# The rests of 25 weight units computed by Pool instead of VectorE in a two-block transformer kernel

## The chip, the cores and the metric

The kernel runs on one core of one Trainium2 chip. The metric is the device time of one execution in microseconds (us). The kernel before has a median of 2389.01 us in 3 runs (2388.89 to 2389.41).

## The reference

Two hybrid transformer layers are applied to one sequence of 512 positions and 1024 channels, all in fp32. The part that matters here is the sparse branch of the first layer's attention, and the projections that are computed beside it:

```python
def hybrid_layer(x, mem, ...):
    x = x + 0.5 * swiglu_ffn(rmsnorm(x, ffn1_norm_g), ffn1_w_in, ffn1_w_out)
    h = rmsnorm(x, mix_norm_g)
    q, kv, nsa_g, conv_in, q_mem, merge_g = jnp.split(h @ w_in, split_points, axis=-1)
    ...
    o_nsa = nsa_attention(q, k_cmp, v_cmp, rmsnorm(ks, k_norm_g), vs, rmsnorm(kw, k_norm_g), vw, gates, rel_bias)
    o_conv = short_gated_conv(conv_in, conv_w, conv_b)
    o_mem = memory_attention(q_mem, mem, mem_norm_g, w_mem_kv, mem_q_norm_g, mem_k_norm_g)
    g_nsa, g_conv, g_mem = jnp.split(jax.nn.sigmoid(merge_g), 3, axis=-1)
    x = x + (g_nsa * o_nsa + g_conv * o_conv + g_mem * o_mem) @ w_out
    return x + 0.5 * swiglu_ffn(rmsnorm(x, ffn2_norm_g), ffn2_w_in, ffn2_w_out)
```

`nsa_attention` has 16 query heads in 4 groups; for each head it forms softmax rows over compressed, selected and windowed keys and adds the three results under gates. A second block (window attention with sinks, gated linear attention, memory attention, feed-forward) follows.

## The kernel before

**A matmul as three.** Activations lie transposed, 128 channels on the partitions and 512 positions in the columns. Weights come as units of 128 x 1024 fp32 numbers (some 768 or 640 wide), 420 of them in the order of their use. Each fp32 operand is used as a rounded half (type fp32r, tile names with H or `hi`) and a rest (value minus rounded half, names with L or `lo`), and a product is high x high + high x rest + rest x high. A dense unit is so 8 x 3 matmuls of 512 columns.

**The road of a unit n.** SyncE loads it into `raw[n % 4]` once TensorE is done with unit n - 4. ScalarE copies it, rounded, to `whi[n % 3]` (L1660) once TensorE is done with unit n - 3. VectorE subtracts, `raw - whi`, and writes the rest to `wlo[n % 4]`, which is the same memory as `raw[n % 4]` (L2099). TensorE waits for both signals in `weights(n)` and uses the unit. Two units with special layout (`STACKED`) go another way.

**The order.** `order()` writes one list `w.items`; each item has a kind (`score`, `turn`, `weigh`, `scale`, `rest`, `values`, `conv`, `tap`, `sq`, `sgate` and so on) and the number of units that are used up to it (`upto`). The order within a stage is written by hand in `TIMES`. Each engine's program goes through the same list and does its own part of each item. ScalarE's and VectorE's programs put `split(n)` ahead of the first item for which `n < upto - 1 + NHI`, NHI = 3, so some two units ahead of use. Engines work in order; across engines they wait for semaphores.

**The sparse stage.** It has 128 tiles (`Head("spa")`, 4 groups x 4 heads x 2 branches x 4 query blocks; a tile of block i is 128 x 128(i + 1)). For tile t: TensorE makes scores (`score`, L1134, 2 matmuls `t_KS,t_QS`); VectorE adds the bias and finds the row minimum into `pp[t % 6]` (`weigh`, L2368); ScalarE takes the exponential and its sum (L1813); VectorE takes the reciprocal (`scale`, L2381); Pool multiplies the rows by it and by a gate (`scale`, L2777); TensorE transposes `pp` (`turn`, L1369), five tiles behind the score; ScalarE copies the rounded half out of the bank (L1660, `t_PS`) and VectorE the rest (`rest`, L2104); at a head's end TensorE multiplies with the values (`values`). Between tiles stand projections, convolution (`conv`, `tap`), gates and the query and key norms of the next group. A norm's inverse square root is a chain of small VectorE instructions on 128 x 16 numbers (`newton`, L2112 to L2124); ScalarE spreads the result (`t_tmp<-t_sn`) and TensorE transposes it (L1209). The normed queries and keys are stacked in halves by ScalarE and VectorE (L2468, L2504).

**Pool** has little else: L2777 and L2780 (scalings), L2785 (`widestat`, sum of two tiles of squares), clears, and the last tile of the result. It issues no DMA of this stage.

Of the kernel before, what the change touches and what calls it, by code (L numbers as in the profile page):

```python
# [10 lines left out]
ALU = mybir.AluOpType  # L11
# [72 lines left out]
UNIT = 1024  # L84
# [3 lines left out]
NHI = 3  # L88
WARM = 6
NRAW = 4  # L90
# [840 lines left out]
STACKED = {"w_ng": (48, 64), "w_alr": (16, 32)}  # L931


def build(nc, A, out):
    stack = ExitStack()
    w = order()
    unit = w.units

    def sb(name, shape, dt=F32):
        return stack.enter_context(nc.sbuf_tensor("t_" + name, shape, dt))[:]  # L940
# [9 lines left out]
    def place(name, at, cols, dt=F32):  # L950

        assert at + cols <= ARENA + NRAW * UNIT
        return nc.alloc_sbuf_tensor_at("t_" + name, [P, cols], dt, offset=base + 4 * at)[:]

    def f32(ap):
        return ap.bitcast(F32)

    raw = [place(f"raw{i}", ARENA + i * UNIT, UNIT) for i in range(NRAW)]
    wlo = [place(f"wlo{i}", ARENA + i * UNIT, UNIT, F32R) for i in range(NRAW)]
    whi = [sb(f"whi{i}", [P, UNIT], F32R) for i in range(NHI)]  # L960
# [101 lines left out]
    def spare(hd, t):  # L1062

        return (pp2 if hd.kind in ("win", "mm2") else pp)[t % RING]
# [10 lines left out]
    def width(hd, i):  # L1075
        if hd.kind == "spa":
            return (i + 1) * P
        return P if hd.kind == "win" and i == 0 else 256
# [11 lines left out]
    def signal(name):  # L1090
        return Signal(stack.enter_context(nc.semaphore("s_" + name)))

    full = signal("bank_full")
    w_hi, w_lo = signal("weight_hi"), signal("weight_lo")
    x_hi, x_lo = signal("operand_hi"), signal("operand_lo")
    evac, copied = signal("bank_evacuated"), signal("bank_copied")
    curve, calc, scaled = signal("curve_applied"), signal("vector_done"), signal("rows_scaled")
    zeroed, cleared, summed = signal("zeroed"), signal("cleared"), signal("squares_summed")
    d_raw = [signal(f"d_raw{i}") for i in range(NRAW)]
    d_half = [signal(f"d_half{i}") for i in range(4)]  # L1100
    d_x = [signal(f"d_x{i}") for i in range(KD)]
    d_m = [signal(f"d_m{i}") for i in range(KD)]
    d_s = [signal(f"d_s{i}") for i in range(KD)]
    d_b = [signal(f"d_b{i}") for i in range(KD)]
    d_o = [signal(f"d_o{i}") for i in range(KD)]
# [10 lines left out]
    def squares(what, h, q):  # L1116
        if what == "k":
            return T[h][:, 256 * q:256 * q + 256]
        return T[q] if h else T[2 + q]
# [9 lines left out]
    def pe_program(e):  # L1129
        on = Once(e)  # L1130
# [20 lines left out]

        def weights(n):
            on.wait_ge(*w_hi.at(n))
            on.wait_ge(*w_lo.at(n))
            return whi[n % NHI], wlo[n % NRAW]

        def first_half(n):
# [21 lines left out]
        def stacked(item, n, ready):  # L1179
            b = take("d", item)  # L1180
            hi, _ = weights(n)
            for k in range(KD):
                operand((*ready, k))
                c = slice(k * P, (k + 1) * P)
                f = two(b, hi[:, c], XH[:, k, :], XL[:, k, :], k == 0, k == KD - 1)
            f.then_inc(*full.tick(item, ("u", n)))
# [900 lines left out]
    def dve_program(e):  # L2087
        on = Once(e)
        parts = {}

        def split(n):
            name, _, width, _ = unit[n]
            on.wait_ge(*w_hi.at(n))
            if name in STACKED:
                m, at = STACKED[name]
                x, hi = (t.rearrange("p (k c) -> p k c", k=KD) for t in (raw[n % NRAW], whi[n % NHI]))
                e.tensor_tensor(hi[:, :, at:at + m], x[:, :, 0:m], f32(hi[:, :, 0:m]), ALU.subtract).then_inc(*w_lo.tick(n))
                return
            e.tensor_tensor(wlo[n % NRAW][:, 0:width], raw[n % NRAW][:, 0:width], f32(whi[n % NHI][:, 0:width]),  # L2099
                            ALU.subtract).then_inc(*w_lo.tick(n))  # L2100
# [657 lines left out]
        n = 2  # L2758
# [7 lines left out]
    def pool_program(e):  # L2766
        on = Once(e)

        def scale(t):
            hd, i = w.tiles[t]  # L2770
            wd = width(hd, i)
            p, r = spare(hd, t)[:, 0:wd], sa[t % RING][:, 4:5]
            on.wait_ge(*calc.at(("rc", t)))
            if hd.kind == "spa":
                on.wait_ge(*calc.at(("gn",)))
                k = 3 * (4 * hd.more["g"] + hd.more["r"]) + 1 + hd.more["a"]
                e.tensor_scalar(p, p, r, gn[:, i, k:k + 1], ALU.mult, ALU.mult).then_inc(*scaled.tick(t))  # L2777
            else:
                on.wait_ge(*d_c.at(0))
                e.tensor_scalar(p, p, r, cst[:, C_ONE:C_ONE + 1], ALU.mult, ALU.mult).then_inc(*scaled.tick(t))  # L2780

        def widestat(what, h):
            a, b = squares(what, h, 0), squares(what, h, 1)
            on.wait_ge(*curve.at(("wsq", what, h, 1)))
            e.tensor_tensor(a, a, b, ALU.add).then_inc(*summed.tick(("wsq", what, h)))  # L2785

        def winload():
            on.wait_ge(*full.at(("ffo", 1, 0, 0)))
            e.memset(lrw, 0.0).then_inc(*cleared.tick("lrw"))

        def hidzero():
            on.wait_ge(*full.at(("memv", 1, 1)))
            for q in range(2):
                e.memset(hk[2 * q], 0.0)
                e.memset(hk[2 * q + 1], 0.0).then_inc(*cleared.tick("hid"))

        def sparsezero():
            on.wait_ge(*full.at(("values", 3)))
            e.memset(f32(VC), 0.0).then_inc(*cleared.tick("sparse"))

        def cclear(g):
            on.wait_ge(*full.at(("values", 3 + 8 * g)))
            for q in range(2):
                e.memset(f32(PCT[q]), 0.0).then_inc(*cleared.tick(("kcp", g)))

        def final(k):
            if k == 7:
                on.wait_ge(*curve.at(("gain", 7)))
                on.wait_ge(*copied.at(("rb", 6)))
                e.tensor_tensor(XT[:, 7, :], XT[:, 7, :], RB, ALU.mult).then_inc(*scaled.tick(("final", 7)))  # L2810

        do = dict(widestat=widestat, winload=winload, final=final, cclear=cclear, scale=scale, hidzero=hidzero, sparsezero=sparsezero)
        for (kind, *args), _ in w.items:
            if kind in do:
                do[kind](*args)

# [80 lines left out]
    def rsq_out(R, nt, n):  # L2897
        return sn[slot[R]][:, 5, 0:nt * n].rearrange("p (i h) -> p i h", i=nt)

    signals = [full, w_hi, w_lo, x_hi, x_lo, evac, copied, curve, calc, scaled, zeroed, cleared, summed, *d_raw, *d_half, *d_x, *d_m, *d_s, *d_b, *d_o,  # L2900
               d_c, d_vec, d_rel, d_oh, d_w2, d_g, *d_tb, d_mask, d_gc, d_lrw]
    for program in (pe_program, act_program, dve_program, pool_program, sp_program):
        program(Count())
# [89 lines left out]
```

## Time and profile before

| what | before |
|---|---|
| median of 3 runs | 2389.01 us (2388.89 to 2389.41) |
| the profiled execution's own time | 2387.31 us |
| its span, first to last instruction | 2385.5 us |
| TensorE (PE) busy | 2354.6 us, 99% |
| VectorE (DVE) busy | 1423.0 us, 60% |
| ScalarE (ACT) busy | 1000.6 us, 42% |
| Pool busy | 164.8 us, 7% |
| mean granted TensorE clock | 0.999 |

The span lies within the execution's own time; the rest of that time is before the first and after the last instruction. Times of rows count from the span's start. A busy TensorE doesn't mean that its rate is the highest possible: consecutive matmuls overlap, so short pauses between them are not seen as idle time. PEld is the load of the stationary operand, beside PE. A row of the table by stretches has: the stretch, its length, then busy us (and count of instructions) of PE, PEld, DVE, ACT and Pool, the granted clock as a share, the DMA share and GB/s. A row of a timeline has: start, duration, engine, line, operation, output<-inputs, shapes, count, and in a bracket how long the engine was idle before and what ended that.

### The profile page before, as it was taken

Reading aid. Unit: us, or ns where it says so; the run is one execution under the profiler, and the core shown is the slowest. Engines: PE = TensorE matmul, PEld = TensorE weight load, DVE = VectorE, ACT = ScalarE, POOL = GpSimd, SP = SyncE. Lnnn points to the kernel's source line nnn. Section 1 sums busy time; section 2 is a strip of 40 time slices with the busy share of each in tenths; the row PEclk is TensorE's granted clock in tenths of the full one; section 3 lists DMA queues with packets and bytes.
Section 4 is the critical chain, followed back from the end, with each engine's and each line's share of the span. In section 5 each row is a group of like instructions: output and inputs, shape, how many; then the busy total and the mean of one; then the engine's idle time right before and its main releaser. Section 6 shows DMA issues by size and latency. Waiting matters only on the chain.

```text
span 2385.5 us, 30247 instructions
## 1 busy us (share of the span) xinstructions
PE 2354.6 (99%) x11480; PEld 1971.6 (83%) x11480; DVE 1423.0 (60%) x2891; ACT 1000.6 (42%) x1852; POOL 164.8 (7%) x251
## 2 busy tenths in 40 slices
PE   9999999999999999999999999999999999999998
PEld 7888888888888888878888888888888887888887
DVE  6435546675658897875434446777654667543444
ACT  5223334442335686653322334665522346322222
POOL 0000000110001233310000000111100001000000
PEclk9999999999999999999999999999999999999999
DMA  4454434332322211222333334211223332323322
GB/s 151 116 124 135 117 117 142 115 106 82 121 93 89 67 59 53 67 91 95 97 95 105 97 109 122 71 54 54 62 88 109 127 110 71 98 88 107 97 87 90
DMA packets 86409, 231.33 MB, mean 97 GB/s; under 512 B 8504, under 2 KB 23480, under 8 KB 86266
## 3 DMA queue, kind: packets, MB, share of 16 engines
q1 hardware_dynamic: 81072, 221.42, 29.7%
q10 hardware_dynamic: 5194, 7.98, 2.1%
q8 instruction: 93, 1.52, 0.3%
q14 instruction: 50, 0.41, 0.1%
HBM read 217.83 MB, written 11.53 MB: 96 GB/s over the span
## 4 chain that ended last, share of the span: by engine, by line
PE 94%; DVE 3%; ACT 2%; issue 1%; DMA 0%; SPq 0%; DVEq 0%; POOL 0%; ACTq 0%
PE bank L1134 91%; PE bank L1369 2%; PE bank L1209 1%; DVE t_pp L2368 0%; ACT t_pw L1813 0%; ACT t_whi L1660 0%; DVE t_wlo L2099 0%; DVE t_PS L2104 0%; DMA t_XT<-in_xT 0%; PE bank L1230 0%; PE bank L1541 0%; ACT t_tmp L1660 0%; DVE t_pw L2368 0%; DVE t_XT L2746 0%; DVE t_PW L2104 0%
## 5 line engine op out<-in xcount | busy, mean ns | idle before, releaser
L1134 PE MATMUL bank<-t_XH,t_whi 128*128 128x512 f32 x2064 | 812.5, 394 | 1.4 <-DVE t_wlo L2099 0.5
L1134 PE MATMUL bank<-t_XL,t_whi 128*128 128x512 f32 x2064 | 803.6, 389 | 0.0
L1134 PE MATMUL bank<-t_XH,t_wlo 128*128 128x512 f32 x2048 | 798.0, 390 | 0.0
L2099 DVE TENSOR_TENSOR t_wlo<-t_raw,t_whi 128x1024 fp32r<-128x1024 f32 (+2 forms) x416 | 477.4, 1149 | 374.5 <-ACT t_whi L1660 371.1
L1660 ACT ACTIVATE t_whi<-t_raw 128x1024 fp32r<-128x1024 f32 (+3 forms) x422 | 416.4, 988 | 414.1 <-PE bank L1134 355.7
L1134 PEld LDWEIGHTS bank<-t_XH,t_whi 128*128 128x128 f32 x2064 | 387.6, 188 | 82.3 <-ACT t_XH L1660 1.5
L1134 PEld LDWEIGHTS bank<-t_XL,t_whi 128*128 128x128 f32 x2064 | 387.8, 188 | 77.1
L1134 PEld LDWEIGHTS bank<-t_XH,t_wlo 128*128 128x128 f32 x2048 | 384.5, 188 | 81.0
L1134 PE MATMUL bank<-t_RX,t_whi 128*128 128x512 f32 x1056 | 325.2, 389 | 0.0
L2227 DVE TENSOR_TENSOR t_tmp<-bank,t_RB 128x512 f32<-128x512 f32 x178 | 122.4, 688 | 195.1 <-PE bank L1134 189.6
L1134 PEld LDWEIGHTS bank<-t_RX,t_whi 128*128 128x128 f32 x1056 | 198.2, 188 | 41.2
L1134 PE MATMUL bank<-t_RX,t_wlo 128*128 128x512 f32 x528 | 205.4, 389 | 0.0
L1660 ACT ACTIVATE t_RX<-t_tmp 128x512 fp32r<-128x512 f32 x66 | 41.7, 632 | 208.8 <-DVE t_tmp L2235 208.8
L1134 PEld LDWEIGHTS bank<-t_RX,t_wlo 128*128 128x128 f32 x528 | 99.1, 188 | 20.5
L2777 POOL TENSOR_SCALAR t_pp<-t_pp,t_sa,t_gn 128x128 f32<-128x128 f32 (+3 forms) x128 | 87.5, 690 | 318.4 <-DVE t_sa L2381 317.6
L1813 ACT ACTIVATE t_pp<-t_pp,t_sa 128x256 f32<-128x256 f32 (+3 forms) x144 | 79.5, 553 | 66.1 <-DVE t_sa L2368 65.4
L2780 POOL TENSOR_SCALAR t_pw<-t_pw,t_sa,t_cst 128x256 f32<-128x256 f32 (+1 forms) x80 | 49.3, 620 | 732.2 <-DVE t_sa L2381 715.9
L1748 ACT ACTIVATE t_tmp<-t_tmp 128x512 f32<-128x512 f32 x66 | 41.7, 632 | 132.5 <-DVE t_tmp L2227 132.5
L1660 ACT ACTIVATE t_XH<-t_XT,t_vec 128x512 fp32r<-128x512 f32 x48 | 34.4, 723 | 108.3 <-DVE t_XT L2248 52.5
L1134 PE MATMUL bank<-t_OA,t_whi 128*128 128x512 f32 x256 | 79.4, 391 | 0.0
L2248 DVE SCALAR_TENSOR_TENSOR t_XT<-bank,t_XT 128x512 f32<-128x512 f32 x47 | 32.5, 692 | 75.1 <-PE bank L1134 75.1
L2104 DVE TENSOR_TENSOR t_RX<-t_tmp,t_RX 128x512 fp32r<-128x512 f32 x66 | 45.7, 693 | 46.0 <-ACT t_RX L1660 46.0
(335 smaller groups left out, 2694.5 us busy)
## 6 DMA issues: line engine op xcount, KB each, us to landing
t_raw<-in_f_in SPq DMA_DIRECT2D x86, 512.0 KB, 3.5
t_raw<-in_f_out SPq DMA_DIRECT2D x32, 384.0 KB, 3.1
t_raw<-in_w_conv SPq DMA_DIRECT2D x24, 512.0 KB, 3.5
t_raw<-in_w_merge SPq DMA_DIRECT2D x24, 512.0 KB, 3.5
t_raw<-in_fg SPq DMA_DIRECT2D x22, 512.0 KB, 3.5
t_raw<-in_fu SPq DMA_DIRECT2D x22, 512.0 KB, 3.5
t_raw<-in_f_out SPq DMA_DIRECT2D x32, 320.0 KB, 3.0
t_raw<-in_w_g SPq DMA_DIRECT2D x16, 512.0 KB, 3.6
```

What stands on the lines that cost most here:

```text
L1134: return e.matmul(o, l, r, start=start, stop=stop, skip_group_check=True)
L1209: f = e.transpose(b[:, i * P:(i + 1) * P], r, ident)
L1369: f = e.transpose(b[:, j * P:(j + 1) * P], spare(hd, t)[:, j * P:(j + 1) * P], ident)
L1660: return e.activation(o, i, ACT.Copy, **how)
L1748: e.activation(s, a, ACT.Silu).then_inc(*curve.tick(("silu", f, h, m)))
L1813: e.activation(p, p, ACT.Exp, scale=-1.0, bias=s[:, 0:1], accum_out=s[:, 1:2]).then_inc(*curve.tick(("ex", t)))
L2099: e.tensor_tensor(wlo[n % NRAW][:, 0:width], raw[n % NRAW][:, 0:width], f32(whi[n % NHI][:, 0:width]), ALU.subtract).then_inc(*w_lo.tick(n))
L2104: e.tensor_tensor(o, x, f32(hi), ALU.subtract).then_inc(*x_lo.tick(item, *more))
L2227: e.tensor_tensor(o, banks[item], RB, ALU.mult).then_inc(*evac.tick(done, ("free", item)))
L2248: e.scalar_tensor_tensor(XT[:, m, :], banks[item], HALF[f], XT[:, m, :], ALU.mult, ALU.add).then_inc(*evac.tick(("free", item), *done))
L2777: e.tensor_scalar(p, p, r, gn[:, i, k:k + 1], ALU.mult, ALU.mult).then_inc(*scaled.tick(t))
L2780: e.tensor_scalar(p, p, r, cst[:, C_ONE:C_ONE + 1], ALU.mult, ALU.mult).then_inc(*scaled.tick(t))
```

## The change

Of the units from the one after the first sparse score up to the last sparse score, all that are 1024 wide and not stacked form a set `pooled`. For these VectorE's `split(n)` returns at once, and Pool's program gets a `split(n)` of its own, at the same places of the list, which waits for ScalarE's rounded half, subtracts, and gives a new signal. TensorE waits for that signal with these units. The instruction and its operands are the same; loads and ScalarE's copies are as before. The set holds units 151 to 175.

```diff
+    scores = [(n, args[0]) for n, ((kind, *args), _) in enumerate(w.items) if kind == "score"]
+    spa = [n for n, t in scores if w.tiles[t][0].kind == "spa"]
+    pooled = {n for n in range(w.items[spa[0]][1] + 1, w.items[spa[-1]][1]) if unit[n][2] == UNIT and unit[n][0] not in STACKED}
...
-    w_hi, w_lo = signal("weight_hi"), signal("weight_lo")
+    w_hi, w_lo, w_pool = signal("weight_hi"), signal("weight_lo"), signal("weight_lo_by_pool")
...
         def weights(n):
             on.wait_ge(*w_hi.at(n))
-            on.wait_ge(*w_lo.at(n))
+            on.wait_ge(*(w_pool if n in pooled else w_lo).at(n))
...
         def split(n):
             name, _, width, _ = unit[n]
+            if n in pooled:
+                return
             on.wait_ge(*w_hi.at(n))
...
+        def split(n):
+            on.wait_ge(*w_hi.at(n))
+            e.tensor_tensor(wlo[n % NRAW], raw[n % NRAW], f32(whi[n % NHI]), ALU.subtract).then_inc(*w_pool.tick(n))
+
         do = dict(widestat=widestat, winload=winload, final=final, cclear=cclear, scale=scale, hidzero=hidzero, sparsezero=sparsezero)
-        for (kind, *args), _ in w.items:
+        n = 2
+        for (kind, *args), upto in w.items:
+            while n < min(upto - 1 + NHI, len(unit)):
+                if n in pooled:
+                    split(n)
+                n += 1
             if kind in do:
                 do[kind](*args)
```

## Rows read from the trace of the kernel before

**Rows 1.** The page of the kernel before, its part on busy time.

```profile
PE 2354.6 (99%) x11480; PEld 1971.6 (83%) x11480; DVE 1423.0 (60%) x2891; ACT 1000.6 (42%) x1852; POOL 164.8 (7%) x251
```

**Rows 2.** Table by stretches of the sparse stage, busy us of each engine.

```profile
737.00:925.00 188.00, 188.00 (x1088) 164.73 (x1087) 154.39 (x448) 132.64 (x329) 51.82 (x77) 1.00 0.21 70
925.00:950.00 25.00, 20.67 (x140) 18.01 (x140) 22.89 (x90) 17.83 (x56) 9.46 (x15) 1.00 0.13 44
950.00:990.00 40.00, 40.00 (x215) 34.30 (x214) 32.51 (x88) 25.50 (x62) 11.74 (x16) 1.00 0.22 73
990.00:1014.00 24.00, 23.70 (x142) 20.40 (x141) 22.14 (x72) 18.38 (x54) 9.34 (x15) 1.00 0.14 44
1014.00:1036.00 22.00, 19.87 (x119) 16.57 (x119) 20.46 (x65) 17.08 (x49) 8.93 (x13) 1.00 0.08 25
```

**Rows 3.** Chain that ended last in 737 to 925 us, its shares by line.

```profile
by line: PE bank L1134 87.7%; PE bank L1369 10.2%; PE bank L1209 1.4%; PE bank L1523 0.5%; PE bank L1512 0.5%
```

**Rows 4.** L2099 in 737 to 990 us: min, median, max ns, and waits.

```profile
L2099 DVE TENSOR_TENSOR t_wlo<-t_raw,t_whi x25: 1205/1225/1577, 736.7 to 988.0; 128x1024 fp32r<-128x1024 f32 x25
...
  ACT t_whi L1660: 11.4, 11
```

**Rows 5.** Timeline of Pool, 375 to 391 us, its two-input instructions.

```profile
375.68 0.74 POOL L2785 TENSOR_TENSOR t_tmp<-t_tmp 128x256 f32<-128x256 f32 x1 [375.24 <-ACT t_tmp L1776]
390.11 1.29 POOL L2785 TENSOR_TENSOR t_tmp<-t_tmp 128x512 f32<-128x512 f32 x1 [13.69 <-ACT t_tmp L1776]
```

**Rows 6.** Timeline of VectorE, 375 to 377 us.

```profile
375.83 0.61 DVE L2201 TENSOR_TENSOR t_rn<-t_rn 128x4 f32<-128x4 f32 x1
```

**Rows 7.** Timelines of three engines around the chain `newton`, 828 to 837 us.

```profile
828.73 1.05 ACT L1660 ACTIVATE t_whi<-t_raw 128x1024 fp32r<-128x1024 f32 x1
...
831.42 0.17 DVE L2124 TENSOR_TENSOR t_sn<-t_sn,t_rn 128x16 f32<-128x16 f32 x1
...
831.99 1.22 DVE L2099 TENSOR_TENSOR t_wlo<-t_raw,t_whi 128x1024 fp32r<-128x1024 f32 x1
...
835.88 1.14 ACT L1660 ACTIVATE t_tmp<-t_sn 128x512 f32<-128x512 f32 x2
...
836.61 0.60 PE L1209 MATMUL bank<-t_cst,t_tmp 128*128 128x128 f32 x4
```

**Rows 8.** Timelines of VectorE, Pool, TensorE around the scaling at 850.71 us.

```profile
849.31 1.23 DVE L2099 TENSOR_TENSOR t_wlo<-t_raw,t_whi 128x1024 fp32r<-128x1024 f32 x1
...
850.71 0.78 POOL L2777 TENSOR_SCALAR t_pp<-t_pp,t_sa,t_gn 128x512 f32<-128x512 f32 x1 [2.39 <-DVE t_sa L2381]
...
852.23 0.49 PE L1369 MATMUL bank<-t_cst,t_pp 128*128 128x128 f32 x3
```

**Rows 9.** Timelines of four engines around two successive rests, 805 to 814.

```profile
805.51 1.06 ACT L1660 ACTIVATE t_whi<-t_raw 128x1024 fp32r<-128x1024 f32 x1
...
806.85 1.05 ACT L1660 ACTIVATE t_whi<-t_raw 128x1024 fp32r<-128x1024 f32 x1
...
811.59 0.45 POOL L2777 TENSOR_SCALAR t_pp<-t_pp,t_sa,t_gn 128x128 f32<-128x128 f32 x1 [11.23 <-DVE t_sa L2381]
...
812.19 0.42 DVE L2368 CUSTOM_DVE_ANT_0 t_pp<-bank,t_TB 128x256 f32<-128x256 f32 x1
...
812.64 0.29 PE L1369 MATMUL bank<-t_cst,t_pp 128*128 128x128 f32 x1
...
814.06 0.48 PE L1134 MATMUL bank<-t_XH,t_whi 128*128 128x512 f32 x1
```

**Rows 10.** Timeline of VectorE at the edges of two stretches.

```profile
918.83 1.23 DVE L2099 TENSOR_TENSOR t_wlo<-t_raw,t_whi 128x1024 fp32r<-128x1024 f32 x1 [2.78 <-ACT t_whi L1660]
...
926.29 0.42 DVE L2368 CUSTOM_DVE_ANT_0 t_pp<-bank,t_TB 128x256 f32<-128x256 f32 x1 [0.32 <-PE bank L1134]
...
990.45 0.69 DVE L2227 TENSOR_TENSOR t_tmp<-bank,t_RB 128x512 f32<-128x512 f32 x1 [1.21 <-PE bank L1134]
```

**Rows 11.** Timeline of VectorE, the pair of copies behind the first moved rest.

```profile
738.02 1.40 DVE L2504 TENSOR_TENSOR t_KS<-t_tmp 64x512 fp32r<-64x512 f32 x2
```

More of the change, by code:

```diff
@@ L2898, in rsq_out @@
         return sn[slot[R]][:, 5, 0:nt * n].rearrange("p (i h) -> p i h", i=nt)
-    signals = [full, w_hi, w_lo, x_hi, x_lo, evac, copied, curve, calc, scaled, zeroed, cleared, summed, *d_raw, *d_half, *d_x, *d_m, *d_s, *d_b, *d_o,
+    signals = [full, w_hi, w_lo, w_pool, x_hi, x_lo, evac, copied, curve, calc, scaled, zeroed, cleared, summed, *d_raw, *d_half, *d_x, *d_m, *d_s, *d_b, *d_o,
                d_c, d_vec, d_rel, d_oh, d_w2, d_g, *d_tb, d_mask, d_gc, d_lrw]
```

## The prediction

> **What bounds the kernel now.** I read the page first: TensorE is busy for 2354.6 of 2385.5 us, VectorE for 1423.0, Pool for 164.8 [rows 1]. So only what makes TensorE wait can move the time much. The change touches one stage, so I then read the table by stretches over that stage, cut where TensorE changes its face [rows 2]. In 737 to 925 us TensorE is busy for 188.00 of 188.00 us; in 950 to 990 for 40.00 of 40.00. It idles 4.33 us in 925 to 950, 0.30 in 990 to 1014 and 2.13 in 1014 to 1036, 6.76 us in all. VectorE is loaded in every one of them (154.39 of 188.00; 22.89 of 25.00), which looks like a second bound, but load is not lateness: the chain of work of 737 to 925 names TensorE's lines alone [rows 3]. There nothing that VectorE does ends last.
>
> Next, where the instructions sit that move. VectorE makes 25 rests (L2099) between 736.7 and 988.0 us, 1225 ns in the middle, and sat idle 11.4 us in 11 of them for ScalarE's rounded half [rows 4]. They are the 25 units 151 to 175 that the new set holds: the window runs from the unit after the first sparse score to the last one, and unit 176 (split at 1003 us) stays on VectorE. So none moves in 990 to 1036.
>
> **What it removes.** 25 x 1.225 = 30.6 us of VectorE's work, and 11.4 us in which its queue stood still at a wait. What is late next? Two of the three stretches with idle TensorE must be asked. Ahead of 925 to 950 the last moved instruction starts at 918.83; at 926.29 VectorE waits 0.32 us for a TensorE score [rows 10]. It had caught up, so a VectorE that is 1.2 us (with the wait before it 4.0 us) earlier waits longer there, and the 4.33 us stay. Ahead of 990 the last one starts at 988.0 [rows 4], and VectorE waits 1.21 us for TensorE at 990.45 [rows 10]. Same answer. The 2.13 us of 1014 to 1036 begin 25 us behind the last moved rest. The gain on the path is taken as 0; its other end is 0.30 us (the idle of 990 to 1014), or 1.1 us if waits hidden by overlapping matmuls there count too (my estimate, taken as some pauses of 0.2 to 0.4 us each).
>
> **What it adds: the price of one rest on Pool.** Pool's only two-input instructions are L2785: 0.74 us for 256 columns, 1.29 for 512 [rows 5], so 2.15 ns a column, and 1024 columns cost about 1.29 + 512 x 0.00215 = 2.39 us. The ends of the cost: 1.23 us (as fast as VectorE), and 4.8 us (twice my value, since subtraction into the rounded type at this width is not in the trace on Pool). I take 2.4, the straight line through the nearest rows. 25 of them make 60 us; Pool's load in 737 to 990 rises from 73 to about 133 of 253 us: room enough on average.
>
> The Trainium skill, "GPSIMD Engine Reference", sections 3.1 and 4.1, advises VectorE for elementwise work and gives 4497 ns for a two-input add of 2048 columns on Pool; half of that would be an estimate of 2.25 us, and the sum below would come out 0.3 us lower. That rule speaks of the instruction's own time; the trace shows TensorE never waiting for these rests, so it doesn't decide here.
>
> **Do the weights come in time?** TensorE needs unit n's rest when it takes unit n. The tightest case is unit 158: its rounded half ends at 805.51 + 1.06 = 806.57, TensorE starts it at 814.06 [rows 9]. Pool would be done at 809.0, 5 us early. Cover is gone only if a rest takes over 7 us. Cost 0. The load into the same buffer waits for TensorE, not for Pool, and SyncE's queue is as before.
>
> **What is queued behind a rest on Pool.** Each rest now waits at its place in Pool's queue for ScalarE's rounded half, and the scalings L2777 behind it wait too; TensorE's transposes L1369 wait for those, and so do VectorE's later reductions into the same buffer. VectorE had the same wait at the same place, so reciprocals behind it came late already. I put 2.4 us on Pool from the end of each of the 25 rounded halves and looked for the next scaling. Most find the queue free. Where two rests follow each other (806.57 and 806.85 + 1.05 = 807.90), Pool ends at 811.4, and the next scaling starts at 811.59 anyway [rows 9]: 0.2 us to spare, and 0.6 between that scaling's end (812.04) and its transpose at 812.64. The one place that is late: the rounded half ahead of 849.31 us. Pool would hold 849.3 to 851.7; the scaling of 850.71 starts 1.0 later and ends at 852.5, its transpose began at 852.23 [rows 8]. TensorE loses 0.4 us. Six more scalings start up to 1.1 us late and by the same reckoning still end before their transposes. Sum: 0.4 us.
>
> **Contention.** VectorE and Pool get in each other's way when VectorE reads two operands out of SBUF: the 128x4 product of VectorE at 375.83, begun 0.15 us after Pool's L2785, took 0.61 us [rows 6], where such an instruction takes 0.17 (831.42) [rows 7]. 375.68 + 0.74 is 376.42; it ended at 376.44. So it stood until Pool was done. An instruction with one input in PSUM did not: 0.42 us at 812.19 under Pool's scalings and 0.42 at 926.29 beside an idle Pool [rows 9, 10]. So a rest on Pool stops VectorE only where VectorE comes to a two-SBUF instruction within those 2.4 us. Most of what it does there reads a bank. Four places remain. Three are copies into stacked halves behind 736.7, 950.8 and 970.8 us, such as the pair at 738.02 [rows 11]: without the rest of 736.67 it would begin at 736.8, and is now held until Pool ends at 738.8, so VectorE is 0.8 us behind there instead of 1.2 ahead. The fourth is at 829.8.
>
> The Trainium skill, "SBUF — State Buffer", section "Who interferes with whom", says that VectorE with two SBUF inputs and a Pool instruction that reads SBUF exclude each other for the whole instruction, the later one being blocked. The trace agrees (0.61 us in place of 0.17). Were it otherwise, the sum below would lack its second term, 0.4 us.
>
> At 829.8 it bites: the rounded half ends at 828.73 + 1.05 = 829.78, in the middle of a chain of small two-input instructions that ends at 831.42 + 0.17 [rows 7]. Pool would stop it until 832.2, so its end moves from 831.6 to 833.7; the rest at 831.99 (1.22) is gone, so VectorE is 0.9 us behind. ScalarE's copies of the result (835.88) and TensorE's spread at 836.61 come after that with nothing between; some of the 0.9 goes in waits. I take 0.4 us for TensorE (ends 0 and 0.9).
>
> **Sum.** 0.4 + 0.4 = 0.8 us on TensorE, less 0, rounded to 1.0 for the three smaller places. The profiled execution took 2387.3 us around its span of 2385.5, so it would become 2388.3; the median of the runs is 2389.0, 1.7 above the profiled one, so I forecast 2390.0 us. That is a change of 0.04%. A measurement of this kernel can tell about 0.2%, 4.8 us, from none.
>
> **Rivals.**
> 1. *VectorE's relief reaches TensorE* (against: it waits for TensorE at 926.29 and 990.45; for: 92% load in both stretches). If only 990 to 1014 profits: 1.1 us off, no contention loss, 2388.0, still within the bound. If the whole 6.76 us fall: 2382.3, faster. The second needs VectorE's lateness to be carried across 926.29, which the row denies.
> 2. *Pool becomes late* (slower). Place: the pair of rests at 806.6 and 807.9 and the scalings behind them. Each us that a rest takes above 2.5 comes twice there (slack 0.6), and once at 850.7 and at a third place. With 3.65 us a rest, 1.9 + 1.7 + 0.7 = 4.3 plus 0.8 for contention: 2394.1; with 4.8, going over the 25 places in the same way, some 15 us: 2404. It passes 0.2% from about 3.6 us a rest. For it: width and type never seen on Pool; against: the straight line.
> 3. *VectorE is held everywhere*, also with one operand in PSUM. Then each rest costs it up to 2.4 instead of 1.2, its load in 737 to 925 becomes 154.4 + 20 x 1.2 = 178 of 188, and some of its 1 us delays reach TensorE: some 5 to 8 us, 2395. Against: 0.42 beside 0.42.
> 4. *The set isn't what I think* (empty, or rests done on both): 2389.0, no change.
>
> **Chances.** Forecast 0.72; rival 1 in its small form 0.12, in its large one 0.02; rival 2 0.08; rival 3 0.03; rival 4 0.03. Faster by over 0.2%: 0.02. Slower by over 0.2%: rival 3 and most of rival 2, 0.09. Same: 0.89. The range: 2387.4 (rival 1's small form and half a us of spread between runs) to 2393.2 (a rest of 3.2 us, with both contention ends). Left out: the large form of rival 1, and most of rivals 2 and 3.
>
> **What would show it.** L2099's place taken by 25 Pool TENSOR_TENSOR t_wlo at 2.4 us (step "price"); Pool about 133 us busy in the stretches up to 990; VectorE 30 us less, but the chain of small instructions near 829.8 with one of about 2.3 us in it; TensorE still without idle in 737 to 925 save for some tenths near 836 and 852; the 4.3 us of idle in 925 to 950 as before. TensorE idle for Pool at a transpose elsewhere, or L2099's successor above 3 us, would make the prediction wrong upward; a 925 to 950 with less idle, downward.

## The result, and the profile after

| | before | after |
|---|---|---|
| median | 2388.95 us (2387.72 to 2389.80, 6 runs) | 2396.23 us (2394.79 to 2398.68, 6 runs) |
| the profiled execution's own time | 2387.31 us | 2394.79 us |
| its span | 2385.5 us | 2393.0 us |
| mean granted TensorE clock | 0.999 | 0.997 |

The change makes the kernel slower: ratio 1.0032, 95% interval 1.0019 to 1.0045. The forecast was 2390.0 with a range up to 2393.2, and "same" with a chance of 0.89. It was wrong by 6 us. In three variants below a single execution lies far from all others (3426.10, 6191.33 and 13554.57 us); their medians are given without it.

The page of after, its busy times (compare [rows 1]):

```profile
PE 2359.9 (99%) x11480; PEld 1975.0 (83%) x11480; DVE 1403.1 (59%) x2866; ACT 999.9 (42%) x1852; POOL 220.9 (9%) x276
```

The work moved as foreseen: VectorE is 20 us less busy, Pool 56 us more. (VectorE's relief is less than 30 us because the operations that stay take 9.8 us longer, see below.) TensorE is 5 us *more* busy with the same 11480 matmuls. The same work in more busy time points to a lower clock, and that was the first hint.

The moved rests in after (least, middle and longest in ns, then first and last start):

```profile
L2819 POOL TENSOR_TENSOR t_wlo<-t_raw,t_whi x25: 2381/2397/2842, 736.6 to 995.6; 128x1024 fp32r<-128x1024 f32 x25
```

Table by stretches of after. Columns as in [rows 2]: stretch, length, busy us and count of PE, PEld, DVE, ACT and Pool, then the granted clock as a share, DMA share and GB/s.

```profile
737.00:755.00 18.00, 17.85 (x87) 14.74 (x85) 10.81 (x27) 10.01 (x24) 11.78 (x10) 1.00 0.27 95
755.00:764.00 9.00, 7.45 (x39) 6.45 (x40) 6.37 (x31) 5.15 (x16) 2.41 (x4) 0.81 0.34 118
764.00:930.00 166.00, 164.81 (x961) 144.26 (x960) 118.45 (x369) 116.54 (x291) 82.81 (x83) 1.00 0.19 63
930.00:957.00 27.00, 23.25 (x146) 20.43 (x144) 24.20 (x94) 18.77 (x58) 9.43 (x15) 0.94 0.11 37
957.00:997.00 40.00, 39.40 (x212) 33.46 (x211) 29.53 (x81) 24.84 (x62) 21.59 (x21) 1.00 0.22 73
```

In [rows 2] TensorE had no idle time at all in 737 to 925. Now 755 to 764 has 1.55 us of it and a granted clock of 0.81, and 930 to 957 has 0.94. Both traces hold the same 11480 matmuls in the same order, so they can be laid side by side: matmul number k of after less matmul number k of before gives TensorE's lateness at each place. Worked out so from the starts of both traces (place in before's time, lateness there in us):

```
place         753   756.5  764    830    837    845    853    922    925    931    945    950    957    1980   2000
after         0.07  2.23   3.78   3.76   3.98   3.98   4.46   4.48   5.65   5.66   6.38   6.37   7.20   7.21   7.46
```

All 7.4 us arise at eight places, in steps: 2.16, 1.55, 0.22, 0.48, 1.17, 0.72, 0.83, 0.25. Nothing lies between. That is not the picture of an engine that is short of time; it is one of single collisions. What stands at them:

**The clears (2.16 at 756, 1.17 at 925).** Pool also sets the two tiles `t_PCT` to zero for each group (item `cclear`, L2804 before, L2809 after). In before, on Pool and then on ScalarE:

```profile
746.58 0.99 POOL L2804 MEMSET t_PCT<- 128x512 f32 x2
748.88 0.49 ACT L1660 ACTIVATE t_PCT<-t_kc 128x128 fp32r<-128x128 f32 x2
```

```profile
913.40 0.99 POOL L2804 MEMSET t_PCT<- 128x512 f32 x2
919.80 0.50 ACT L1660 ACTIVATE t_PCT<-t_kc 128x128 fp32r<-128x128 f32 x2
```

The clears were done 1.3 and 5.4 us before ScalarE came to copy into these tiles; nobody waited. The timelines of Pool, ScalarE and TensorE in after:

```profile
749.05 2.39 POOL L2819 TENSOR_TENSOR t_wlo<-t_raw,t_whi 128x1024 fp32r<-128x1024 f32 x1 [1.76 <-ACT t_whi L1663]
751.38 0.99 POOL L2809 MEMSET t_PCT<- 128x512 f32 x2
752.46 0.51 ACT L1663 ACTIVATE t_PCT<-t_kc 128x128 fp32r<-128x128 f32 x2 [3.49 <-POOL t_PCT L2809]
755.30 0.74 PE L1137 MATMUL bank<-t_KS,t_QS 128*128 128x512 f32 x2 [0.45 <-DVE t_PS L2109]
757.58 1.92 PE L1137 MATMUL bank<-t_cst,t_tmp 128*128 128x2 f32 x16 [1.25 <-DVE t_PS L2109]
```

```profile
919.36 2.40 POOL L2819 TENSOR_TENSOR t_wlo<-t_raw,t_whi 128x1024 fp32r<-128x1024 f32 x1 [1.41 <-ACT t_whi L1663]
923.36 2.40 POOL L2819 TENSOR_TENSOR t_wlo<-t_raw,t_whi 128x1024 fp32r<-128x1024 f32 x1 [1.60 <-ACT t_whi L1663]
925.71 0.98 POOL L2809 MEMSET t_PCT<- 128x512 f32 x2
926.72 0.51 ACT L1663 ACTIVATE t_PCT<-t_kc 128x128 fp32r<-128x128 f32 x2 [2.33 <-POOL t_PCT L2809]
```

Pool waited for ScalarE's rounded half of unit 153 (1.76 us), made the rest (2.39 us) and only then cleared: done at 752.37 instead of 747.57, 4.8 us later. ScalarE stood 3.49 us in its own queue for the clear, and everything behind that copy came late: the copies of `t_PS`, then VectorE's L2109, then two waits of TensorE, 0.45 and 1.25 us. The clear of group 2 stands behind two rests, units 169 and 170, and ScalarE waited 2.33 us for it. At the clears of groups 1 and 3 the lateness takes no step.

**Half clock (1.55, 0.72, 0.25).** Table of three stretches of after:

```profile
759.57:762.98 3.41, 3.41 (x10) 2.72 (x9) 2.77 (x18) 0.67 (x3) 0.51 (x1) 0.50 0.01 2
940.48:943.89 3.41, 3.41 (x16) 3.11 (x14) 2.98 (x9) 2.04 (x6) 0.24 (x1) 0.50 0.28 82
1991.79:1995.20 3.41, 3.26 (x15) 2.93 (x15) 2.56 (x15) 3.05 (x14) 2.46 (x6) 0.50 0.01 2
```

The granted clock is 0.50 in them, TensorE's lower level of 1.2 GHz. The first lies right behind the two waits above. The other two lie at waits that before has as well: in before's time 1.51 us up to 933.91, and 0.84 and 1.08 us up to 1983.15 and 1984.73. The profiled execution of before has no such stretch until its last matmuls.

**Contention and a late scaling (0.22, 0.48, 0.83).** At 830 and 853 as predicted. VectorE's instruction in the chain, then, at 957, VectorE, Pool and TensorE:

```profile
833.72 2.32 DVE L2126 SCALAR_TENSOR_TENSOR t_sn<-t_sn 128x16 f32<-128x16 f32 x1
...
957.26 2.40 POOL L2819 TENSOR_TENSOR t_wlo<-t_raw,t_whi 128x1024 fp32r<-128x1024 f32 x1 [1.54 <-ACT t_whi L1663]
958.22 3.07 DVE L2473 TENSOR_TENSOR t_QS<-t_tmp 64x512 fp32r<-64x512 f32 x2 [0.87 <-ACT t_tmp L1663]
962.67 0.33 PE L1372 MATMUL bank<-t_cst,t_pp 128*128 128x128 f32 x1 [0.60 <-DVE t_sa L2373]
```

In before the same pair took 1.76 us:

```profile
952.17 1.76 DVE L2468 TENSOR_TENSOR t_QS<-t_tmp 64x512 fp32r<-64x512 f32 x2
```

It is two-input work out of SBUF, and Pool was in a rest until 959.66. With VectorE's instructions of the two traces laid side by side in the same way, only five take over 0.3 us longer in after: one at each of the four places that the prediction named (2.0 us behind 736.7, 2.1 at 830, 1.3 behind 950.8, 1.6 behind 970.8) and a product at 984 (0.4). All five read two operands out of SBUF. They are 7.4 of the 9.8 us; of the three pairs only the one at 957 makes TensorE late.

### The profile page after: what moved, and what is told of

Same layout as the page of the kernel before. It is cut to its first block, busy times and chain, and to the rows that moved or that the text cites. A ratio compares the mean times of both kernels' runs of the same rounds, so it can differ in the third digit from the quotient of the medians.

```text
span 2393.0 us, 30247 instructions
## 1 busy us (share of the span) xinstructions
PE 2359.9 (99%) x11480; PEld 1975.0 (83%) x11480; DVE 1403.1 (59%) x2866; ACT 999.9 (42%) x1852; POOL 220.9 (9%) x276
## 4 chain that ended last, share of the span: by engine, by line
PE 93%; DVE 3%; ACT 2%; issue 1%; POOL 1%; DVEq 0%; ACTq 0%
PE bank L1137 90%; PE bank L1372 2%; PE bank L1212 1%; ACT t_whi L1663 0%; DVE t_pp L2373 0%; POOL t_wlo L2819 0%; DVE t_wlo L2104 0%; ACT t_tmp L1663 0%; ACT t_pw L1816 0%; DVE t_PS L2109 0%; ACT t_pp L1816 0%; PE bank L1233 0%; PE bank L1544 0%; DVE t_pw L2373 0%; DVE t_OC L2605 0%
## 5 line engine op out<-in xcount | busy, mean ns | idle before, releaser
L2104 DVE TENSOR_TENSOR t_wlo<-t_raw,t_whi 128x1024 fp32r<-128x1024 f32 (+2 forms) x391 | 446.4, 1144 | 362.1 <-ACT t_whi L1663 359.1
L2109 DVE TENSOR_TENSOR t_PS<-bank,t_PS 128x128 fp32r<-128x128 f32 (+3 forms) x128 | 60.9, 485 | 22.8 <-ACT t_PS L1663 21.8
```

The lines of the kernel that those rows point to most:

```text
L2109: e.tensor_tensor(o, x, f32(hi), ALU.subtract).then_inc(*x_lo.tick(item, *more))
```

## The experiments

Four theories ran against each other. **A**: the clears, queued behind rests, are the main loss. **B**: the clock falls by the shifted time alone. **C**: contention of VectorE and Pool, spread over all 25 rests. **D**, formed last: TensorE's pause makes its clock fall. (The expectations of clears_first and three_units call B what is C here, and that of shift33 calls C what is B here.) Each ratio is against before on the same chip, measured beside the variant: before had a median of 2388.26 us beside the first four variants, 2387.83 beside the next four, 2387.96 beside unit_153_filled, after_filled, after_again and before_again, and 2388.16 beside the last two. "Lateness" is that of the table above, against the first trace of before.

**clears_first.** The changed kernel, with the two clears ahead of the rests in Pool's program:

```diff
+        early = {153: 0, 169: 2}
 ...
+                if n in early:
+                    cclear(early[n])
                 if n in pooled:
                     split(n)
 ...
-            if kind in do:
+            if kind in do and (kind != "cclear" or args[0] not in early.values()):
```

> The changed kernel, but Pool clears PCT for groups 0 and 2 ahead of the rests of units 153 and 169, as it did before the change. Theory A (the clears, queued behind a rest on Pool, hold ScalarE and then TensorE: 1.9 us of delay at 754 us and 1.1 at 924, and a stretch at the lower clock behind the first): some 3 to 5 us of the 7.3 come back, 2391 to 2393 us. Theory B (the 25 rests cost by their number: Pool's price and VectorE held by the shared operand read): the clears are a bystander, the time stays within 1 us of 2396. Both leave 0.4 us at the scaling near 852 and 0.8 at the copies near 958.

Measured: 2389.70 us, ratio 1.0006 (0.9997 to 1.0015). Pool and ScalarE around the first clear:

```profile
747.12 0.98 POOL L2809 MEMSET t_PCT<- 128x512 f32 x2
748.94 2.40 POOL L2819 TENSOR_TENSOR t_wlo<-t_raw,t_whi 128x1024 fp32r<-128x1024 f32 x1 [0.84 <-ACT t_whi L1663]
748.76 0.49 ACT L1663 ACTIVATE t_PCT<-t_kc 128x128 fp32r<-128x128 f32 x2
```

ScalarE waits no more. With all 25 rests still on Pool, 1.4 us above before are left; 5.9 of the 7.3 are back, where 3 to 5 were expected. That is more than the clears' own 3.3 us: the stretches at half clock behind 757 and 931 us are gone as well (only the one near 1990 is there, 0.2 us). That the one behind 931 is gone may be chance: later traces have it in some kernels without a late clear (late_units, clears_first_22) and not in others. Lateness is zero up to 830, and then it takes steps of 0.21 by 837, 0.48 by 853 and 0.83 by 957: the three other places, unchanged.

**three_units.** Only the three rests ahead of the two clears go to Pool: `pooled = {153, 169, 170}`.

> Only units 153, 169 and 170 have their rest on Pool, the ones that stand ahead of a clear; the other 22 are back on VectorE. Theory A: these three carry the loss of 1.9 and 1.1 us and what the clock adds, 2392 to 2395 us. Theory B: three of 25 rests cost a tenth of 7 us, 2389 to 2390.

Measured: 2394.02 us, ratio 1.0022 (1.0013 to 1.0031). Three of the 25 rests bring 5.8 us. Its trace: 2.35 late at 756.5, 3.05 more by 764, 1.16 at 925, nothing at 837, 853 or 957.

**late_units.** Only two rests of the end of the stage, 1003 us and later: `pooled = {176, 177}`. It asks what VectorE's relief is worth where TensorE is idle.

> Only units 176 and 177 have their rest on Pool (before: on VectorE at 1003 and 1019 us); they stand just ahead of the one stretch, 1014 to 1036 us, where VectorE ends last and a rest lies within the same burst. If a relief of VectorE can reach TensorE at all it is here: up to 1.2 us faster, 2388. If TensorE's idle time there comes from the order of the last tiles alone: 2389.0.

Measured: 2388.70 us, ratio 1.0002 (0.9993 to 1.0011). No gain, and by its trace TensorE is no earlier at 1028 than it was at 957.

**shift33.** The kernel before, with 33 more matmuls in a dense item of the first feed-forward part, so that all later work comes later and nothing else changes:

```diff
+                if item == ("ffb", 0, 0, 4) and k == 0:
+                    for _ in range(33):
+                        mm(b[:, 0:cols], hi[:, 0:P], xh[:, 0, :], True, True)
```

> The kernel before with 33 more matmuls of 512 columns in one dense item near the start (their results are overwritten), which moves all that follows by 33 x 0.228 = 7.5 us and changes nothing else. Theory C (whether TensorE's clock falls behind one of the kernel's pauses depends on the moment at which the pause comes, so that a mere delay can bring stretches at the lower clock): the time is above 2389.0 + 7.5 = 2396.5 by 1.6 us for each such stretch, and the profile shows one or more at places that had none, near 934 + 7.5 or 1984 + 7.5 us. Against it (the clock falls only behind pauses that the change made or lengthened): 2396.5, no stretch at the lower clock.

Measured: 2396.30 us, ratio 1.0033 (1.0021 to 1.0045), 8.0 us above before, of which 33 x 0.227 = 7.5 are the added matmuls. Moving the work in time costs 0.5 us by the medians, which is within the interval. Its trace has half clock behind three pauses that before has (at 943, 1038 and 1994 us, 3.41 us each), none at 757. So B fails as an explanation of 757.

**unit_153** and **units_169_170.** The clears one by one: `pooled = {153}`, `pooled = {169, 170}`.

> Only the rest of unit 153 goes to Pool, in the changed kernel's place, one item ahead of the clear of group 0. Theory A (the clears queued behind rests): the changed kernel's matmuls were 1.93 us late after this clear and lost 1.6 us more where the clock stood at half; so 1.9 to 3.5 us, 2390.2 to 2391.8 by the kernel before on this chip (2388.3). Theory B (the clock falls by the shifted time alone): no more than 1 us. Theory C (many small losses by contention of VectorE and Pool over all 25): no more than 0.3 us. In the trace of A, ScalarE waits some 3.5 us for t_PCT near 749 to 752, and the next matmuls of line 1137 start 1.9 us later than before.

> Only the rests of units 169 and 170 go to Pool, ahead of the clear of group 2. Theory A: 1.1 us at 924 to 929, with or without up to 1.6 us of half clock in the pause that follows at 932 to 940: 2389.4 to 2391.0 by 2388.3 before. Theories B and C: within 0.3 us. Together with unit_153 alone, A wants the two losses to add up to about that of three_units (5.8 us by the medians), whatever the clock takes of it.

Measured, each without its one far execution: 2394.19 us, ratio 1.0024 (1.0014 to 1.0034), and 2390.20 us, ratio 1.0009 (1.0001 to 1.0018). A single instruction moved from one engine to another costs 6.4 us. The expectation for it, 1.9 to 3.5 us, was too low. Where it goes, by TensorE's rows and the table by stretches of unit_153:

```profile
755.92 0.73 PE L1137 MATMUL bank<-t_KS,t_QS 128*128 128x512 f32 x2 [0.55 <-DVE t_PS L2109]
758.19 2.47 PE L1137 MATMUL bank<-t_cst,t_tmp 128*128 128x2 f32 x16 [1.26 <-DVE t_PS L2109]
```

```profile
752.00:759.37 7.37, 5.56 (x33) 4.46 (x32) 2.53 (x9) 5.33 (x14) 3.38 (x7) 1.00 0.42 144
759.37:766.19 6.82, 6.82 (x25) 6.05 (x25) 4.06 (x23) 2.93 (x12) 1.20 (x2) 0.50 0.02 5
```

The clear makes TensorE wait 1.81 us; then it runs 6.82 us at half clock and loses 3.1 us more (lateness 0.59 at 753, 2.88 at 756.5, 5.98 at 764), and 0.9 in the pause behind 931. The pair 169 and 170 loses 1.17 us at 925, as in after, and 0.4 at half clock near 1990. The two single losses (6.4 and 2.4) add up to 8.7, where three_units lost 5.8, so the sum that was expected did not come. The pauses add by the traces (2.2 and 1.2 us in three_units too); what differs is the clock's part. The intervals of the three ratios are wide enough for the two sums to be equal, so no more is shown.

**clear_0_late.** The kernel before with no rest moved. Only Pool's queue is occupied ahead of the first clear:

```diff
             on.wait_ge(*full.at(("values", 3 + 8 * g)))
+            for k in range(16 if g == 0 else 0):
+                e.memset(f32(PCT[0]), 0.0).then_inc(*cleared.tick(("again", k)))
+                on.wait_ge(*cleared.at(("again", k)))
             for q in range(2):
```

> The kernel before with no rest moved: Pool only sets t_PCT0 to zero 16 times more ahead of the clear of group 0, one behind the other, 0.53 us or more each, 8.5 to 9.6 us in all. Theory A: the clear's end decides, and beyond some 2.9 us of slack (it came 4.8 us later in the changed kernel and cost 1.93) every microsecond of lateness is one of the span: 5.6 to 6.7 us late near 757, and up to 3.2 us more where the clock falls in the longer pause (three_units showed 6.83 us at half clock there): 2393.9 to 2398.2 by 2388.3 before. If it is the rest itself (its reading of t_raw and t_whi, or contention with VectorE) and not its place in Pool's queue: under 1 us.

Measured: 2397.39 us, ratio 1.0041 (1.0029 to 1.0053). Pool, ScalarE, TensorE:

```profile
746.90 9.29 POOL L2804 MEMSET t_PCT<- 128x512 f32 x16
756.25 0.99 POOL L2807 MEMSET t_PCT<- 128x512 f32 x2
757.33 0.51 ACT L1660 ACTIVATE t_PCT<-t_kc 128x128 fp32r<-128x128 f32 x2 [8.03 <-POOL t_PCT L2807]
758.96 1.11 PE L1369 MATMUL bank<-t_cst,t_pp 128*128 128x128 f32 x4 [4.30 <-ACT t_tmp L1660]
762.45 1.84 PE L1134 MATMUL bank<-t_cst,t_tmp 128*128 128x2 f32 x8 [0.52 <-DVE t_PS L2104]
```

```profile
757.82:771.47 13.65, 11.89 (x43) 10.26 (x44) 6.60 (x31) 7.72 (x24) 3.04 (x6) 0.50 0.08 30
```

The clear ends at 757.24 here and at 752.98 in unit_153; less what the two executions were behind at 753 (0.33 and 0.59) it is 4.52 us later. The matmuls of two columns (755.37 in before) start 6.75 us late here and 2.23 us late there, by the same deduction: 4.52 us. So beyond some 2.6 us of slack (4.82 - 2.23) each microsecond of the clear is one of TensorE's, and the rest itself, its reads or its contention have no part in it. The half clock lasts 13.65 us here and begins at 757.82, within the wait of 4.30 us. That a longer pause brings a longer stretch is not shown by one execution: behind waits of 1.6 to 1.8 us there are stretches of 3.41 us (after), 6.82 (unit_153) and 10.24 (after_filled, below).

**clears_first_22.** As clears_first, and units 161, 162 and 171, whose rests stand at the three remaining places, stay on VectorE.

> As clears_first, and the rests of units 161, 162 and 171 stay on VectorE. In clears_first's trace matmuls fell behind by 0.2 us at 836 (VectorE's line 2126 took 2.32 us instead of 0.17 beside the rest of unit 161), by 0.4 us at 852 (a scaling behind the rest of unit 162) and by 0.9 us at 957 (two operations of line 2473 took 3.07 us instead of some 1.8 beside the rest of unit 171). If these are the whole of what was left, the time is that of the kernel before, 2388.3, within 0.5 us, and 22 rests on Pool gain nothing; if the relief of VectorE is worth something once no loss covers it, up to 1 us less; if the loss is spread over the rests, still some 1.2 us more.

Measured: 2388.98 us, ratio 1.0001 (0.9993 to 1.0010). The lateness against before at 830, 837, 853, 925 and 957 moves only by the 0.6 us that a stretch at half clock near 937 costs (0.26, 0.26, 0.28, 0.26, 0.86). Between them TensorE gains and loses less than 0.1 us. So by the trace the three places are the whole of the rest, C is true of two of them alone (the third is a late scaling), and 22 rests off VectorE bring nothing. The times alone could not say so: by the medians 22 rests are 1.15 us above before, more than the 0.5 expected, by the ratio 0.2 us, and both lie within the interval. It is the best form of this change that I found, and it does not beat the kernel before.

**What makes the clock fall.** In clears_first there is neither a pause at 757 nor half clock; in unit_153 there are both. To part the pause from everything else that a late clear brings, the pause was to be filled with work.

unit_153_filled and after_filled put five unused matmuls of 512 columns ahead of the wait at 758.19:

```diff
         def sqstat(g):
+            b = take("s", ("sqstat", g)) if g == 1 else None
+            for _ in range(5 if g == 1 else 0):
+                mm(b, XH[:, 0, 0:P], XH[:, 0, :], True, True)
             on.wait_ge(*curve.at(("sqsq", g, 1)))
```

> unit_153 with 5 matmuls of 128x512 that nothing uses, in the bank of the 16 matmuls of two columns and ahead of the wait for ScalarE's squares (1.26 us in unit_153's trace; 5 by 0.227 us are 1.14 us, so they cost nothing there). unit_153 was 6.5 us above before by the medians, of which its trace puts 1.9 on the late clear and the rest on stretches at half clock, the first of 6.83 us behind this wait. Theory D (TensorE's pause makes its clock fall): with the pause filled the clock stays up there and the time is 2389.8 to 2391.0 by 2387.8 to 2388.3 before. If the clock falls for another reason (the few columns of the 16 matmuls, the moment alone), it stays at 2393 to 2396.

> The changed kernel with the same 5 unused matmuls ahead of the same wait (1.25 us in its trace). By theory D it loses the late clears (3.0 us), contention and the late scaling (1.2 us) and now and then a half-clock stretch elsewhere (up to 2 us), not the one at 757 to 766: 2391.5 to 2394. If the filling changes nothing: 2395 to 2397.

Measured: 2393.1 us without the one far execution, ratio 1.0021 (1.0012 to 1.0031), and 2396.01 us, ratio 1.0034 (1.0021 to 1.0046). They don't decide what they were made for. TensorE's row of unit_153_filled says why:

```profile
757.65 1.43 PE L1137 MATMUL bank<-t_XH 128*128 128x512 f32 x5 [1.17 <-DVE t_PS L2112]
```

The wait is for the bank, which VectorE's L2112 (L2109 above) had not yet read, and not for the squares. So the five came behind the pause instead of into it, and cost their own time. The profile's releaser had named VectorE all along; I had read the code and not the row.

Yet they show something else. The waits are as long as in unit_153 (0.55 and 1.17 us), and the trace has the same 6.82 us at half clock. But four of the ten executions took 2390.8 to 2391.6 us at a mean clock of 0.998 or 0.999. Pause and added matmuls make TensorE 3.4 us late there, which on before's fastest 2387.3 us gives 2390.7; 3.1 us more of half clock have no room in these four. So a whole pause does not always bring such a stretch, and the pause is not all that decides: it may be what TensorE does behind it, or the moment at which it comes.

unit_153_dense5 and before_dense5 put the five at the head of the dense item that runs from 749 to 755, ahead of both waits, in unit_153 and in the kernel before:

```diff
+                if item == ("sq", 1, 1) and k == 0:
+                    for _ in range(5):
+                        mm(b[:, 0:cols], hi[:, 0:P], xh[:, 0, :], True, True)
```

> unit_153 with 5 unused matmuls of 128x512 at the head of the dense item that runs from 749 to 755 us, in front of the two waits (0.55 and 1.26 us). ScalarE is late by t_PCT there until some 757.9, whatever TensorE does, so 1.14 us more of matmuls should be absorbed by the waits. Theory D (the pause makes the clock fall): less than 1 us of pause is left, the clock falls more rarely, some executions lie at 2389.5 to 2391 with a clock of 0.998 or more, and the median is below unit_153's 2394.4. If the clock falls for another reason than the pause: 2394 to 2396, no execution below 2393.

> The control: the kernel before with the same 5 unused matmuls in the same place. No wait stands behind them there, so they cost their own 1.14 us: 2389.0 to 2389.5 by 2388.0 before, with a stretch at half clock at 757 in none. If it comes to 2392 or more, the moment or the shift makes the clock fall there, and no pause is needed.

Measured: unit_153_dense5 2392.03 us, ratio 1.0016 (1.0007 to 1.0025); before_dense5 2389.16 us, ratio 1.0005 (0.9996 to 1.0013). TensorE in the two:

```profile
757.62 2.56 PE L1137 MATMUL bank<-t_cst,t_tmp 128*128 128x2 f32 x16 [0.92 <-DVE t_PS L2112]
```

```profile
756.44 1.90 PE L1134 MATMUL bank<-t_cst,t_tmp 128*128 128x2 f32 x16
```

The pause fell from 1.81 to 0.92 us, and the kernel with five more matmuls lies 3.9 us above its before, where unit_153 lies 6.4 above its own: it is 2.5 us *faster*. Its profiled execution (2394.05 us) still has 6.82 us at half clock behind the pause; that others escape is read from their times and clocks. Six of its eleven executions have a mean clock of 0.998 or more and 2390.3 to 2392.0 us, the other five 0.997 and 2392.8 to 2394.1; unit_153's seven all have 0.996 or 0.997 and 2393.2 to 2395.1. The control costs its matmuls (1.0 us against 1.14), and its trace has no pause there and no half clock there; even its slowest execution, 2390.57 us, has no room for 3.1 us more. So D holds in this form: half clock at 757 stands in every trace with the pause (after, after_again, after_filled, three_units, clear_0_late and all three with unit_153 alone) and in none without it (clears_first, clears_first_22, units_169_170, late_units, shift33, before_dense5 and both of before). That half the pause makes the clock fall less often is likely, not shown: unit_153_filled had the whole pause and escaped in four of ten executions, this one in six of eleven, and unit_153, which escaped in none of seven, ran on another chip.

after_again and before_again are the two kernels once more.

> The changed kernel once more, beside after_filled on the same chip and for a second look at its clock. 2394.8 to 2398.7 as measured; the same late matmuls at 754, 924 and 957 within 0.1 us (they are the program's), but stretches at half clock that need not stand at the same pauses (theory D: the pauses are the program's, whether the clock falls in one depends on when it comes).

> The kernel before, unchanged, for a second look at its clock. Its first trace has no stretch at half clock before the last matmuls, but late_units, whose matmuls run at the same times, had three of 3.41 us, at 937, 1032 and 1988 us. Theory D: the kernel before has them too in some executions, in these same three pauses, each costing up to 1.7 us, which would be the whole of its spread of 2387.1 to 2390.1. If its trace shows none again and its time is below 2388, this stays likely, not shown.

Measured: after_again 2396.32 us, ratio 1.0032 (1.0019 to 1.0044); before_again one execution, 2389.22 us. The steps of after_again's lateness are those of after (2.14 at 756.5, 1.57 by 764, 0.21, 0.48, 1.18 at 925, 0.83 at 957), save for the clock's: 0.1 instead of 0.7 behind 931, and 0.9 behind 1028, where after had none. Before_again has half clock at 1029 and at 1989 us, and none at 937. Table by stretches of before_again, then the first of these stretches in the first trace of before:

```profile
1029.50:1032.90 3.40, 3.19 (x12) 2.80 (x13) 2.64 (x13) 2.33 (x10) 2.45 (x5) 0.50 0.00 0
1988.64:1992.04 3.40, 3.40 (x18) 3.02 (x17) 3.15 (x19) 3.29 (x13) 2.42 (x5) 0.50 0.00 0
```

```profile
1029.50:1032.90 3.40, 3.21 (x20) 2.47 (x21) 3.37 (x14) 3.34 (x12) 2.59 (x5) 1.00 0.00 0
```

The same program, the same stretch: 12 matmuls begin in it at half clock, 20 at full clock. Ahead of it TensorE waits the same 0.8 us for `t_PS` in both executions. Of the 1.9 us between the two, 1.7 arise at these two stretches.

## Why the prediction was wrong, step by step

- **TensorE bounds the stage, and VectorE's relief is worth nothing**: right. clears_first_22 takes 22 rests off VectorE and gains nothing (1.0001); late_units takes two more off it just ahead of a stretch with idle TensorE, with as little gain (1.0002). Rival 1 falls in both its forms.
- **The price of a rest on Pool, 2.4 us**: right. L2819 takes 2381 to 2842 ns, 2397 in the middle, 25 times, from 736.6 to 995.6 us. The straight line through the two narrower rows [rows 5] held. Rival 2, which needed 3.6 us, falls; but its kind, Pool late for a follower, is what happened, by queueing and not by price.
- **The weights come in time**: right. TensorE waits for no rest of Pool's.
- **What is queued behind a rest on Pool**: wrong, and this is the step that failed. The text looked for the next *scaling* (L2777) behind each of the 25 rests and for nothing else. Pool's queue also holds the clears (L2804), named in the description of the kernel. They have two followers that matter, ScalarE's copy and all that is behind it in ScalarE's queue. The scalings were right: one late place, 0.4 us foreseen, 0.48 measured; Pool was free for the others, the pair at 806 too. The two clears cost 2.16 + 1.17 = 3.3 us by themselves. The missing question was: which *other* kinds of instruction does the engine have in this window, how late may each be (1.3 us of lead at 748, 5.4 at 919), and what stands behind the one who waits for it.
- **Contention**: the mechanism right, one size wrong. The chain near 830 has its operation of 2.32 us (0.17 before), as foreseen, and costs 0.22 us for 0.4. Of the three pairs of copies that together were rounded to 0.2 us, the one behind 950.8 cost 0.83: there TensorE waits for VectorE's reduction behind the pair (0.60 us at 962.67), which the prediction did not follow up. Its reading that one input in PSUM is not held stands: Pool's scalings of [rows 9] are three that end at 813.32, so they do cover VectorE's 0.42 us at 812.19.
- **The clock**: no term at all. It took 1.55 + 0.72 + 0.25 = 2.5 of the 7.4 us of the profiled execution. The first is a consequence of the clear of group 0: it stands in every trace with a late clear, and not in that of clears_first. The others belong to pauses that both kernels have. The sum counted each wait of TensorE at its own length.

Together: foreseen terms 0.7 for 0.8; the under-sized one 0.83 for 0.2; the forgotten one 3.3; its consequence through the clock and the clock's own scatter 2.5. Rival 3 (VectorE held everywhere) would have been slower by 5 to 8 us, the right size for a wrong reason: with clears_first all rests are on Pool and 1.4 of the 7.3 us are left, and of VectorE's instructions only the five with two SBUF operands took over 0.3 us longer.

The Trainium skill, "SBUF — State Buffer", section "Who interferes with whom", says that the later of two such instructions is blocked until the first is done. The trace agrees once more: when the pair began at 958.22, Pool's rest had 1.44 us to go, and the pair took 1.31 us longer than in before (3.07 for 1.76). The prediction had this rule and used it; what it lacked was the follower at 957.

What stays open: why a given pause brings one stretch at half clock in one execution and a longer one, or none, in another, and how much of it is the pause's length and how much what follows it. It was not forced; shift33, unit_153_filled and the repeated kernels only show that it varies. Also not tried was a kernel before with its own three pauses filled.

## What to carry to other kernels

When work is put into an in-order queue, list every kind of instruction that is queued behind it, the rare ones first (clears, presets, one-off copies): in before, note when each ends, when its reader starts, and what else is in that reader's queue. One moved instruction with 1.3 us of lead behind it cost more than the 24 others together. And price a wait of TensorE in a stretch where it had none at its length and up to three us more (3.1 in unit_153).

## What the runs showed of the hardware that was not expected

- A pause of TensorE can cost more than itself. In unit_153 two waits of 1.81 us in all, between matmuls and 16 matmuls of two columns, were followed by 6.82 us at a granted clock of 0.50 and a loss of 3.1 us; in clear_0_late, with 4.82 us of waits, half clock lasted 13.65 us. With 0.92 us of wait six of eleven executions had no such loss, but neither had four of ten with 1.72 us and five matmuls of 512 columns behind (unit_153_filled). Without a wait no trace has half clock there.
- The scatter of the kernel before is partly the clock. Of its 26 executions beside unit_153 those with a mean clock of 0.999 took 2387.1 to 2387.9 us, those with 0.997 took 2388.6 to 2389.9. A single trace (the first one of before, with no stretch at half clock) is the good end of this scatter, which the prediction could not see.
- The Trainium skill, "TensorE: Matmul & The Clock Gate", section "What's actually happening", says that the observation of TensorE's activity runs freely and does not start with the kernel, so that the moment of a change of clock varies. The two traces of before agree as far as they go: the same waits near 1029 us, half clock behind them in one execution and full clock in the other.
- A two-input subtraction into the rounded type on Pool takes 2.4 us for 128 x 1024, on the line of its additions of 256 and 512 columns [rows 5].
